# A decoder trunk on one core: later rounding of the output weights, a copy moved to GpSimd, and output products that wait for one token tile

## The reference

```python
# layer 0
mix = nsa_mixer(h, ...)            # q, kc, vc, ks, vs, kw, vw, gates = split(h @ w_in_a)
                                   # q_rot = q with the first 16 of 64 dims of each head rotated
                                   # compressed branch uses q, selected and sliding branches q_rot
                                   # out = (gated sum of three attentions) @ w_out_a
h = layer_norm(ALPHA * h + mix); h = layer_norm(ALPHA * h + dense_swiglu(h))
# layer 1
mix = swa_sink_mixer(h, ...)       # 16 heads, 2 kv heads, window 128, a sink per head; @ w_out_b
h = layer_norm(ALPHA * h + mix); h = layer_norm(ALPHA * h + moe_swiglu(h))   # top 2 of 8 experts
```

## Time and profile before

| | us |
|---|---|
| median of 3 runs | 1547.89 |
| lowest and highest of them | 1546.62 and 1548.94 |
| the profiled execution | 1549.21 |
| its span, first to last instruction | 1547.5 |

### The profile page before, as it was taken

How to read it: one execution, slowest core, us unless ns; L and a number is a source line. 1 busy time by engine, 2 the same in 40 slices (tenths; PEclk the granted TensorE clock), 3 DMA queues, 4 the chain that set the end, 5 groups by cost and what they waited for, 6 DMA issues and landing times.

```text
span 1547.5 us, 20331 instructions
## 1 busy us (share of the span) xinstructions
PE 1484.4 (96%) x7441; PEld 1235.0 (80%) x7441; DVE 1205.6 (78%) x1076; ACT 967.4 (63%) x894; POOL 58.5 (4%) x86
## 2 busy tenths in 40 slices
PE   6999989999889799999999999999999999999995
PEld 5866789998766588888888888888888888888884
DVE  5666475554754799899889889889989889988988
ACT  4554434443344377677777777777777777777774
POOL 1012300000012100000000000000000000000000
PEclk9989989999989899999999999999999999999997
DMA  9660045555620689999999999999999999999990
GB/s 338 161 194 1 28 166 188 190 166 197 182 82 28 244 314 345 347 368 347 367 354 342 377 345 362 359 344 364 353 339 364 356 352 355 354 377 344 337 348 27
DMA packets 200921, 425.78 MB, mean 275 GB/s; under 512 B 10384, under 2 KB 42160, under 8 KB 200880
## 3 DMA queue, kind: packets, MB, share of 16 engines
q1 hardware_dynamic: 196864, 419.65, 75.4%
q10 hardware_dynamic: 4016, 5.56, 1.1%
HBM read 424.14 MB, written 1.05 MB: 275 GB/s over the span
## 4 chain that ended last, share of the span: by engine, by line
PE 88%; DVE 6%; ACT 4%; issue 1%; DMA 1%; ACTq 0%; DVEq 0%
PE bank L902 25%; PE bank L904 25%; PE bank L903 25%; PE bank L1095 2%; PE bank L919 2%; PE bank L1252 2%; PE bank L1126 2%; ACT wh L843 2%; PE bank L1313 2%; DVE wl L1344 1%; DVE wl L1800 1%; ACT wh L632 1%; ACT L843 1%; DVE h L1635 1%; DVE pre L1626 1%
## 5 line engine op out<-in xcount | busy, mean ns | idle before, releaser
L902 PE MATMUL bank<-wh,arena_r 128*128 128x512 f32 x1432 | 565.5, 395 | 1.3 <-DVE wl L1800 1.3
L1800 DVE TENSOR_TENSOR wl<-ring,wh 128x2048 fp32r<-128x2048 f32 x224 | 511.9, 2291 | 65.0 <-ACT wh L843 64.9
L904 PE MATMUL bank<-wl,arena_r 128*128 128x512 f32 x1432 | 558.4, 390 | 0.0
L903 PE MATMUL bank<-wh,arena_r 128*128 128x512 f32 x1432 | 558.3, 390 | 0.0
L843 ACT ACTIVATE wh<-ring 128x2048 fp32r<-128x2048 f32 x224 | 428.9, 1918 | 91.7 <-PE bank L904 91.6
L902 PEld LDWEIGHTS bank<-wh,arena_r 128*128 128x128 f32 x1432 | 269.0, 188 | 60.1 <-DVE wl L1800 6.3
L904 PEld LDWEIGHTS bank<-wl,arena_r 128*128 128x128 f32 x1432 | 268.9, 188 | 57.4
L903 PEld LDWEIGHTS bank<-wh,arena_r 128*128 128x128 f32 x1432 | 269.2, 188 | 53.8
L1344 DVE TENSOR_TENSOR wl<-ring,wh 128x2048 fp32r<-128x2048 f32 (+1 forms) x64 | 144.5, 2264 | 110.4 <-ACT wh L632 110.4
L632 ACT ACTIVATE wh<-ring 128x2048 fp32r<-128x2048 f32 (+1 forms) x64 | 120.6, 1892 | 119.7 <-PE bank L904 115.9
L1800 DVE TENSOR_TENSOR wl<-arena,wh 128x2048 fp32r<-128x2048 f32 x64 | 146.7, 2292 | 20.4 <-ACT wh L843 20.3
(11 more groups left out here) (233 smaller groups left out, 1379.2 us busy)
## 6 DMA issues: line engine op xcount, KB each, us to landing
ring<-in_moe_w_in_dram SPq DMA_DIRECT2D x171, 1024.0 KB
ring<-in_moe_w_out_dram SPq DMA_DIRECT2D x56, 1024.0 KB
arena<-in_moe_w_out_dram SPq DMA_DIRECT2D x40, 1024.0 KB, 6.5
slot<-in_moe_w_in_dram SPq DMA_DIRECT2D x32, 1024.0 KB, 6.9
arena<-in_moe_w_in_dram SPq DMA_DIRECT2D x24, 1024.0 KB, 6.7
ring<-in_dense_w_in_dram SPq DMA_DIRECT2D x22, 1024.0 KB
slot<-in_moe_w_out_dram SPq DMA_DIRECT2D x16, 1024.0 KB, 6.2
ring<-in_dense_w_out_dram SPq DMA_DIRECT2D x11, 1024.0 KB
```

Source lines behind the costliest of these rows:

```text
L902: pe.matmul(out_, lh, rh, start=start, stop=False, skip_group_check=True)
L903: pe.matmul(out_, ll, rh, start=False, stop=False, skip_group_check=True)
L904: return pe.matmul(out_, lh, rl, start=False, stop=stop, skip_group_check=True)
L1800: dve.tensor_tensor(wl[:, n % SPLITS, :], slot_at[SLOT[k % PER_EXPERT]], wh[:, n % SPLITS, :].bitcast(F32), ALU.subtract).then_inc(split, 1)
```

## The change

Three things are edited.

1. The three roundings inside an attention move. ACT: from i = 1, 3, 27 to i = 10, 16, 27 in the first attention, from 1, 3, 13 to 6, 12, 13 in the second. DVE: from 1, 3, 27 to 12, 18, 28, and from 1, 3, 13 to 8, 13, 14.
2. The copy of the unrotated query dims (four instructions in all: two before the first attention, two in it at i = 4 and 5) goes from DVE, which read it from PSUM, to POOL, which reads it from the left half of `stage`. PE's transposes of the queries wait for it on a new semaphore, `staged_p`. In POOL's list the late two stand ahead of the weighting of jobs 4 and 5.
3. `mix_part` of tile tt 0 waits for one tile's `heads_out`, that of tt 1 for the second; before, both were waited for ahead of the first.

```diff
+ROUND_A, SPLIT_A = (10, 16, len(JOBS_A) + 1), (12, 18, len(JOBS_A) + 2)
+ROUND_B, SPLIT_B = (6, len(JOBS_B), len(JOBS_B) + 1), (8, len(JOBS_B) + 1, len(JOBS_B) + 2)
...
+            def copy_unturned(j):
+                s = stage[:, j % 2, :].rearrange("p (a g d) -> p a g d", a=2, d=HD)
+                pool.wait_ge(staged_a, j + 1)
+                pool.tensor_copy(s[:, 1, :, ROT:], s[:, 0, :, ROT:]).then_inc(staged_p, 1)
+            for tt in range(NT):
+                copy_unturned(len(PROJ_A) - 2 * NT + tt)
...
+                    if jobs is JOBS_A and i in STAGED_A:
+                        copy_unturned(len(PROJ_A) - NT + STAGED_A.index(i))
...
 # ACT, attention
-                    if i in (1, 3, len(jobs) + 1):
-                        split_weights(n_out + 1 + (1, 3, len(jobs) + 1).index(i))
+                    if i in at:
+                        split_weights(n_out + 1 + at.index(i))
...
 # PE, turn_projection
                 elif kind in ("q0", "q1"):
+                    pe.wait_ge(staged_p, j + 1 - len(PROJ_A) + 2 * NT)
...
 # PE, attention
-                    if i == len(jobs):
-                        pe.wait_ge(heads_out, acc_base + 2)
                     if len(jobs) <= i < len(jobs) + NT:
+                        pe.wait_ge(heads_out, acc_base + 1 + i - len(jobs))
...
 # DVE, stage_part
-                    dve.tensor_copy(dst[:, :, :, ROT:],
-                                    src[:, :].rearrange("p (b r d) -> p b r d", b=2, r=4)[:, :, :, ROT:])
...
 # DVE, attention
-                    if i in (1, 3, len(jobs) + 1):
-                        split_weights(n_out + 1 + (1, 3, len(jobs) + 1).index(i))
+                    if i in at:
+                        split_weights(n_out + 1 + at.index(i))
```

More of the change, by code:

```diff
@@ L306, in decoder_kernel @@
         staged_v = sem("staged_v")
+        staged_p = sem("staged_p")
         cmp_sum = sem("cmp_sum")
@@ L766, in attention @@
                 accs = acc_base
+                at = ROUND_B if swa else ROUND_A
                 for i in range(len(jobs) + LAG_V + 1):
-                    if i in (1, 3, len(jobs) + 1):
-                        split_weights(n_out + 1 + (1, 3, len(jobs) + 1).index(i))
+                    if i in at:
+                        split_weights(n_out + 1 + at.index(i))
                     if i < len(jobs):
@@ L1533, in attention @@
             def attention(jobs, base, mbase, of_jobs, n_out, swa, heads, along):
+                at = SPLIT_B if swa else SPLIT_A
                 for i in range(len(jobs) + LAG_V + 1):
-                    if i in (1, 3, len(jobs) + 1):
-                        split_weights(n_out + 1 + (1, 3, len(jobs) + 1).index(i))
+                    if i in at:
+                        split_weights(n_out + 1 + at.index(i))
                     if i < len(jobs):
```

## The result

| | before | after |
|---|---|---|
| median us | 1548.41 | 1540.44 |
| lowest to highest | 1546.13 to 1551.56 | 1538.14 to 1541.82 |
| profiled execution, its span | 1547.5 | 1540.0 |

The ratio is 0.9948, with a 95% interval of 0.9937 to 0.996: 8.0 us faster (6.2 to 9.8). The forecast was 1541.6, with 1538.7 to 1545.8 as its range. The sum behind it was 6.3 us, so the sign and most of the size are right.

The account below looks back on a forecast made before the run. PE was taken as the bound nearly everywhere, so time won ahead of the expert loop counts in full. The terms, -3.1 - 4.4 + 0.2 + 1.3 - 0.3 = -6.3 us, took 1547.9 to 1541.6, range 1538.7 to 1545.8.

Parts of the forecast that it names:

- Start of the second attention, -3.1: Without rounding and subtraction there, the maxima of job 3 and PE's transposes come 3.1 us earlier; bounds 1.55 and 3.5.
- Output product, -4.4: Second attention, tile tt 0: the 2.65 us gap goes and twelve matmuls run at full clock; -4.4 us, bounds -3.4 and -4.5.
- DVE has two subtractions now in rounds 13 and 14 ..., ahead of the move of job 11: Second attention's end: two subtractions of 2.29 us, about 484.9 to 489.5, done in time for the product's half 1.
- Subtraction in round 8, +0.2: Second attention: job 7's weights come about 2.2 us later, delaying PE's transpose of job 7; +0.2 us, bounds 0 and +0.5.
- Roundings out of the first attention's start, 0: First attention: DVE and ACT were ahead of PE there, so removing them gains 0, at most 0.3 us.
- Subtraction in round 12, +1.3: First attention: POOL gets job 11 later and PE stalls at its transpose; +1.3 us, bounds 0 and +1.6.
- Rival 1: First attention, round 14: the stall brings the clock down shortly, 3.4 us at half clock, 1.7 us: 1543.3; chance 0.20.
- rival 4: First attention: the round 12 subtraction is absorbed, so no +1.3: 1540.3 us; chance 0.10.
- Rival 2: First attention, round 14: the clock falls at the stall and stays low 13.7 us, costing 6.85: 1548.4 us; chance 0.13.
- rival 3: First attention: the clock falls after both moved subtractions, rounds 12 and 18, so slower: 1555.3 us; chance 0.04.
- Copy on POOL, -0.3: First attention: DVE loses 0.47 us ahead of job 5's maxima, POOL's copy takes 1.2; -0.3 us, bounds -0.5 and +0.3.
- The ratio of 1.96: GpSimd's time over VectorE's for a two-input add; by it POOL's copy takes 1.1 us, leaving the sum the same.

Follow-up runs that it names:

- x_round_a: Kernel before with only the first attention's roundings moved as in the change: 1550.82 us, ratio 1.0013.
- y_after: The changed kernel measured again, on a second occasion: 1539.45 us, ratio 0.9939 to the kernel before.
- x_late_third: The changed kernel with DVE's third subtraction of the second attention at round 15 in place of 14: 1540.81 us, ratio 0.9946 to before.
- x_one_input: The changed kernel with DVE's subtractions of rounds 13 and 14, second attention, replaced by one-input scalings by zero: 1536.01 us, a single look.
- y_best: The changed kernel with DVE's first subtraction of the first attention at round 8, last of the second at 15; second occasion: 1536.62 us, 0.9931 to before.
- x_copy: Kernel before with only the copy of the unrotated query dims moved from DVE to POOL: 1544.33 us, ratio 0.9979.

## Why the prediction was right, point by point

- **Start of the second attention, -3.1.** 3.15 us in the ledger up to the scores of job 5, with the mechanism as told. What it had not: the half clock behind it. It held that the rise comes after the same work (gain 3.1) or at the same time (1.55). It came earlier, after 10.3 us for 17.0, for another 2.6 us. Over all profiles the stretch is 10.2 to 13.7 us in the eight with this edit (mean 11.1) and 13.6 to 17.1 in the six without (mean 15.4), half of the 4.3 between them being 2.1. The edit alone gave 4.2, beyond the bound of 3.5, which its interval (2.8 to 5.7) takes in.
- **Output product, -4.4.** -4.50 in the ledger, -5.0 alone. The product starts behind the values of job 6, at full clock, and no fall follows. Of its steps, "half 1 of the product, at about 490.4, finds its item split" held too.
- **"DVE has two subtractions now in rounds 13 and 14 ..., ahead of the move of job 11"** was costed at nothing. This step failed. It looked at DVE's own list and left out POOL, whose weighting of job 11 runs at that time and is held by DVE (6.07 us for 1.82): +1.13 in the ledger. The same hold in round 18 of the first attention (3.50 us for two) opened no gap, as forecast.
- **Subtraction in round 8, +0.2.** +0.14.
- **Roundings out of the first attention's start, 0.** x_round_a gives no sign of a gain; the 1.08 us gap of the earlier trace rows stands in the profile after as it was, at 106.19.
- **Subtraction in round 12, +1.3.** +1.25, a gap of 1.17 us released by POOL, as worked out from the earlier trace rows. Rival 1 (clock down for 3.4 us, +1.7) came true in the profiled execution to the tenth, and rival 4 fell. Over five profiles with this stall the clock fell behind it in three, for 3.4 (after), 3.4 (y_after) and 6.9 us (x_late_third), and not in x_round_a and x_one_input. Up to this place x_one_input has the same lists as after, so the forecast and rival 1 can both come of the same instructions; both profiles of after itself show rival 1. Rival 2's 13.7 us never came, nor rival 3's second gap, in round 18.
- **Copy on POOL, -0.3.** The size is wrong twice. A copy takes 0.50 us, not 1.2; that changed nothing, since the rotation ends later. The 0.47 us won on DVE bring 3.3 us (1.7 to 4.8). The prediction's words were "the gain of 0.47 is at half clock, so part of it is lost if the rise stays at 122.0": it took the fall at 108.3 as given. In an execution of that kind this is right, as the fall comes ahead of the copy; what it left out are those in which PE comes to the late transpose at full clock, and there the 0.47 us go with whether the clock falls (two falls of two with the gap of 1.23 us, none of five with 0.76). The bound of -0.5 was too near by 2.8 us. The profiled execution of after fell at 107.7 all the same, so it shows only -0.4 there (-0.66 less the -0.25 that stood at 106.19 already).
- **The ratio of 1.96** for elementwise work on GpSimd (the Trainium skill, GPSIMD Engine Reference, section 3.1) spoke against this move. The page has it from an add of two inputs, and it was no guide to this copy of one: 0.50 us from SBUF on POOL, 0.56 from PSUM on DVE.
- **The sum.** The parts alone add up to 10.5 us (-5.0, -4.2, +2.0, -3.3) against 8.0 together. The hold on POOL, +1.1, arises only together; the other 1.4 are within the intervals, and the clock's gains need not add. The change was worth 8.0 us where the sum said 6.3. That the two agree so far has luck in it: the sum left out gains of clock (2 to 3 us), and also a stall (1.1) and a fall (1.7 in some executions), which go the other way. That the median is only 1.2 off the forecast has a further reason: before's median was 1548.4 this time, not 1547.9.

## What to carry to other kernels

Before an instruction of two microseconds that works from SBUF to SBUF is moved on VectorE, look at what GpSimd does at the new place: a scaling of 0.92 us there can come out 4 us later, and PE waits for it. Half a microsecond taken off one wait of PE can be worth several where the clock may fall behind it, so the value of a short edit is measured over ten or more executions with their clocks, not read from one trace. Try each edit of a bundle by itself: here one of the four was a loss inside a gain.

## What was not expected of the hardware

- VectorE and GpSimd hold each other. GpSimd's pair of scalings took 2.86, 3.94 and 6.07 us for 1.82, and VectorE's rotated copies of 64 elements 0.45 and 0.53 us for 0.22 beside GpSimd's. An fp32 instruction of 1.25 us with one input from SBUF does it too; maxima and copies from PSUM do not.
- Identical lists on PE run through different stretches at half clock. The lengths seen in the attentions are 3.4, 6.8 to 6.9, 10.2 to 10.3, 13.6 to 13.7 and 17.0 to 17.1 us. What sets the end of a stretch is not shown by these runs.
- The fall does not follow from the length of one gap alone: it came behind gaps of 1.08 and 1.17 us in some executions and not in others, and gaps of 1.95 us passed without one in y_best, x_late_third, x_one_input and x_copy (there the fall came only 5 us later).
